# A two-block transformer kernel on one core: function table loaded early, small row tables moved later, last store in two halves

## The reference, cut to what matters

```
h = rmsnorm(x, g_pre_mix)                       # start of block 1
proj = h @ w_in                                 # split into q, six k/v parts, gates, ...
kb = k[:, blk] + pos[None, None, :, None, :]    # compressed keys and values: position rows added
...
x = x + rmsnorm(ff, mlp_norm_post[1])           # end of block 2; x is the output
```

## Time and profile before

| | us |
|---|---|
| median of 3 runs | 2114.84 |
| lowest, highest | 2113.89, 2118.77 |
| the profiled execution | 2114.21 |
| its span, first to last instruction | 2112.5 |
| PE busy in the span | 2076.6 |
| DVE busy | 1055.0 |
| ACT busy | 831.1 |
| POOL busy | 256.2 |

### The profile page before, as it was taken

The page is one execution under the profiler, slowest core; times in us unless marked ns, Lnnn a source line. Parts: engine busy times, 40 slices in busy tenths (PEclk is TensorE's granted clock), DMA queues, the critical chain, the costliest instruction groups (busy, mean ns, idle before and its releaser), DMA issues.

```text
span 2112.5 us, 27223 instructions
## 1 busy us (share of the span) xinstructions
PE 2076.6 (98%) x10878; PEld 1717.9 (81%) x10878; DVE 1055.0 (50%) x1782; ACT 831.1 (39%) x1539; POOL 256.2 (12%) x306
## 2 busy tenths in 40 slices
PE   8999999999999999999999999999999999999998
PEld 7987567888887888888888888888877779888887
DVE  5543756565555344665666433333655555334333
ACT  4154765343333234423335322322445554223222
POOL 7400000000000000223321000000433111000000
PEclk9999999999999999999999999999999999999999
DMA  6335512333333222222112223222332222332222
GB/s 163 84 116 87 68 40 81 100 101 100 86 95 100 100 100 90 90 67 74 60 61 80 94 97 100 100 100 100 110 102 89 70 81 90 100 98 94 89 99 80
DMA packets 172347, 191.95 MB, mean 91 GB/s; under 512 B 22882, under 2 KB 141965, under 8 KB 172221
## 3 DMA queue, kind: packets, MB, share of 16 engines
q1 hardware_dynamic: 168301, 176.30, 26.3%
q0 software_dynamic: 3904, 13.90, 3.5%
q10 hardware_dynamic: 16, 0.00, 0.0%
HBM read 182.84 MB, written 7.34 MB: 90 GB/s over the span
## 4 chain that ended last, share of the span: by engine, by line
PE 92%; DVE 4%; ACT 2%; issue 1%; POOL 1%; DMA 0%; POOLq 0%; ACTq 0%; DVEq 0%
PE bank L2463 25%; PE bank L2361 12%; PE bank L2362 12%; PE bank L2363 12%; PE bank L2400 2%; PE bank L2919 2%; PE bank L2401 2%; PE bank L2402 2%; PE bank L2954 1%; PE bank L2956 1%; PE bank L2955 1%; PE bank L2975 1%; PE bank L2615 1%; PE bank L2977 1%; PE bank L2976 1%; PE bank L2631 1%
## 5 line engine op out<-in xcount | busy, mean ns | idle before, releaser
L1577 DVE TENSOR_TENSOR WHL<-raw,WHL 128x1024 fp32r<-128x1024 f32 x309 | 393.5, 1275 | 475.8 <-ACT WHL L967 475.6
L967 ACT ACTIVATE WHL<-raw 128x1024 fp32r<-128x1024 f32 x309 | 325.2, 1054 | 526.5 <-PE bank L2463 338.1
L2361 PE MATMUL bank<-HXh,WHL 128*128 128x512 f32 x1136 | 448.5, 395 | 0.0
L2363 PE MATMUL bank<-HXh,WHL 128*128 128x512 f32 x1136 | 443.6, 390 | 0.0
L2362 PE MATMUL bank<-HXl,WHL 128*128 128x512 f32 x960 | 374.2, 390 | 0.0
L2463 PE MATMUL bank<-WHL,HXh 128*128 128x512 f32 x1344 | 362.3, 390 | 0.0
L2463 PEld LDWEIGHTS bank<-WHL,HXh 128*128 128x128 f32 x1344 | 251.6, 188 | 52.8 <-issue 1.2
L2361 PEld LDWEIGHTS bank<-HXh,WHL 128*128 128x128 f32 x1136 | 213.8, 188 | 48.2 <-issue 4.0
L2363 PEld LDWEIGHTS bank<-HXh,WHL 128*128 128x128 f32 x1136 | 213.6, 188 | 45.1
L2362 PEld LDWEIGHTS bank<-HXl,WHL 128*128 128x128 f32 x960 | 180.5, 188 | 36.0
L2463 PE MATMUL bank<-WHL,HXl 128*128 128x512 f32 x672 | 208.6, 390 | 0.0
(11 more groups left out here) (327 smaller groups left out, 3257.7 us busy)
## 6 DMA issues: line engine op xcount, KB each, us to landing
raw<-in_mlp_w_up_dram SPq DMA_DIRECT2D x64, 512.0 KB, 4.7
raw<-in_mlp_w_down_dram SPq DMA_DIRECT2D x64, 512.0 KB, 4.2
raw<-in_w_up_dram SPq DMA_DIRECT2D x44, 512.0 KB, 5.1
raw<-in_a_w_in_dram SPq DMA_DIRECT2D x32, 512.0 KB, 4.5
raw<-in_w_in_dram SPq DMA_DIRECT2D x24, 512.0 KB, 4.6
raw<-in_w_down_dram SPq DMA_DIRECT2D x22, 512.0 KB, 4.2
raw<-in_w_kv_dram SPq DMA_DIRECT2D x16, 512.0 KB, 4.2
rel_dram<-GB POOLq DMA_DIRECT2D x1, 5120.0 KB, 54.8
```

The source lines that it names most:

```text
L967: return a.activation(dst, src, ACT.Copy, **k)
L1577: v.tensor_tensor(dst(1), src, dst(0).bitcast(F32), ALU.subtract).then_inc(w_lo, 1)
L2361: m.matmul(b[:, :], w[0][:, k, :], x[0][:, k, :], start=(k == 0), stop=False)
L2363: return m.matmul(b[:, :], w[1][:, k, :], x[0][:, k, :], start=False, stop=(k == KD - 1))
```

## The change

Five edits in three places.

1. ScalarE makes a one-column Square into a scratch tile (`junk`) right after `consts`, before it waits for X. The wait for `consts` leaves `norm_tile`.
2. SyncE issues `row_tables()` ahead of slot 3 and no longer ahead of slot 2.
3. TensorE makes the five transposes of `stage` after the four groups of `q` and no longer before them.
4. VectorE splits up to `unit_at["q", 3]` (unit 5) before it waits for those transposes. The copy, the four additions and `split(unit_at["q", 3] + HL)` (units 6 to 8) stand behind as before.
5. The sum of the last tile is made by column halves, and each half is stored by a transfer of its own.

```diff
+        table_in, last_half = sem("table_in"), sem("last_half")
...
             for n, (name, i, parts) in enumerate(slots[:last]):
-                if n == RAW:
+                if n == RAW + 1:
                     row_tables()
...
-            for tt in range(TT):
+            for tt in range(TT - 1):
                 sp.wait_ge(x_ready, 4 * (len(NORMS) - 1) + tt + 1)
                 sp.dma_start(out[0, tt * P:(tt + 1) * P, :], X[:, tt, :]).then_inc(stored, 16)
-            sp.wait_ge(stored, 16 * TT)
+            sp.wait_ge(last_half, 1)
+            sp.dma_start(out[0, T - P:T, 0:HALF], X[:, TT - 1, 0:HALF]).then_inc(stored, 16)
+            sp.wait_ge(x_ready, 4 * len(NORMS))
+            sp.dma_start(out[0, T - P:T, HALF:D], X[:, TT - 1, HALF:D]).then_inc(stored, 16)
+            sp.wait_ge(stored, 16 * (TT + 1))
...
                 if n == 0:
-                    if tt == 0:
-                        act.wait_ge(consts, 1)
                     act.wait_ge(x_tile_in[tt], 16)
...
+            act.wait_ge(consts, 1)
+            a.activation(junk[:, 0:1], negh[:, 0:1], ACT.Square).then_inc(table_in, 1)
             norm_tile(0, 0)
...
-                    v.scalar_tensor_tensor(out=X[:, tt, :], in0=yg[:, tt % 2, :], scalar=yr[:, tt:tt + 1],
-                                           in1=X[:, tt, :], op0=ALU.mult, op1=ALU.add).then_inc(x_ready, 1)
+                    for c in (slice(0, HALF), slice(HALF, D)) if (r, tt) == (6, TT - 1) else (slice(0, D),):
+                        v.scalar_tensor_tensor(out=X[:, tt, c], in0=yg[:, tt % 2, c], scalar=yr[:, tt:tt + 1],
+                                               in1=X[:, tt, c], op0=ALU.mult,
+                                               op1=ALU.add).then_inc(x_ready if c.stop == D else last_half, 1)
...
             split(unit_at["kv01", 1] + HL)

+            split(unit_at["q", 3])
             vec.wait_ge(ps_free["act"], 2)
             vec.wait_ge(consts, 1)
             cols_copy(1)
...
             half_product(0, 1, 1)
+            split_features("q", 4, None, pair(True))
             pe.wait_ge(rows_in, 16 * N_ROWS)
             c = 0
             for i, n in enumerate((C_CONV, CUT, CUT, CMP_L, CMP_L)):
                 ins = m.transpose(bank[4][:, c:c + n], stage[0:n, i, :], ident[0:n, 0:n])
                 c += n
             ins.then_inc(cols_psum, 1)
-            split_features("q", 4, None, pair(True))
             split_features("kv24", 2, None, pair(True))
```

## The result

| | kernel before | changed kernel |
|---|---|---|
| median of 8 runs each | 2113.97 us | 2121.55 us |
| range of the runs | 2112.02 to 2118.77 | 2120.64 to 2126.88 |
| profiled execution, its span | 2114.21, 2112.5 | 2120.64, 2118.9 |

The ratio is 1.0040 (95% interval 1.0031 to 1.0049): the change costs 7.6 us. The forecast was 2120.4, 5.6 above the median known then.

What follows compares the result with a forecast made beforehand. TensorE, busy 98% of the span, was taken as the bound. Start -0.9, new wait with GpSimd and clock +7.9, earlier waits -0.8, end -0.6: +5.6, from 2114.84 to 2120.4 us, range 2117.0 to 2124.5.

Steps and rivals of the forecast that it cites:

- The bound and the place of the loss: Whole kernel: TensorE bounds it, busy 98% of the span; it would wait ahead of `kv24` for VectorE's unit 6.
- The wait: TensorE ahead of `kv24`: 5.9 us for copy, additions and one subtraction, plus 0.7 for GpSimd; sign: 6 to 7 idle.
- The third rival: VectorE's additions before `kv24`: two or more GpSimd selects get between; wait near 10, +9.2 us, time 2124.0; chance 0.14.
- The clock: TensorE after the `kv24` wait: granted clock falls to half somewhere from 51 to 58; +1.3 us, bounds 0 and 2.5.
- What is late next: TensorE after `kv24`: no further unit late, first earlier wait gone and half the second; -0.8 us, bounds -1.1 and 0.
- the old waits: TensorE's waits for VectorE in the kernel before: 0.58 us for unit 9, 0.52 for the evacuation of `kv35`.
- Edit 1: Start, ScalarE: the 1.28 us table load goes under X's transfer; first evacuation at about 10.3; -0.9 us, bounds -1.3 and 0.
- Edit 2: SyncE's queue: slot 3 issued at about 29.5, its first use at 40.21, so no wait; 0 us.
- Edit 5: End, last sum and store in halves: half the transfer saves 0.65, second sum some 0.05 later; -0.6 us, bounds -0.7 and -0.3.
- The total: Whole kernel: all terms sum to +5.6 us, from 2114.84 to 2120.4; chance 0.52.
- The bare wait: Rival at `kv24`: wait just 5.9, no loss to GpSimd or clock; +3.3 us, time 2118.1, within no change; chance 0.25.

Runs made afterwards that it cites:

- the middle alone: Changed kernel without the early table load and the split store at the end (edits 2, 3 and 4 only): 2123.81 us, ratio 1.0050.
- a wait at unit 9: Changed kernel with VectorE splitting up to unit 8, not only unit 5, before it waits for the transposes: 2115.72 us, ratio 1.0013.
- the masks moved: Changed kernel with GpSimd starting its mask loop only when unit 6 is split: 2117.83 us, ratio 1.0021.
- filled kernels: Changed kernel with 30 or 38 unread 512-column products on TensorE between the transposes and the wait for unit 6: 2121.53 and 2121.77 us.
- the two ends alone: Kernel before with only the early table load and the split store at the end (edits 1 and 5): 2112.63 us, ratio 0.9994.

## Why the prediction was right, and where its terms were off

- **The bound and the place of the loss** were right. The loss is one wait of TensorE ahead of `kv24`, ended by VectorE's subtraction of unit 6, as forecast from the order of the queue; moving the units ahead of the wait removed it.
- **The wait** was the mis-sized term. Forecast 5.9 and 0.7 for GpSimd, measured 9.03, outside the 6 to 7 us that the prediction gave as its sign. The bare part measured 5.49, GpSimd's 3.5 and not 0.7. I had judged by the four additions of the earlier trace rows, which hardly lost beside GpSimd (one took 1.35, the others 1.00 to 1.02); but what ran beside them there was tensor_scalar work, not selects. The row that did bear on it was unit 7's 3.56 beside a select. The third rival had this mechanism and its size, at 4: its wait of near 10 is closer to 9.03 than my 6.6, and its +9.2 a little closer to the measured +7.6 than my +5.6. Its argument against itself, that GpSimd would have the longest selects behind it, was wrong: GpSimd itself came 3.5 us earlier than before (its select of 3.67 at 40.96 in place of 44.46), and the two longest mask selects, 2.13 and 2.12, fell on the additions.
- **The clock**: forecast 1.3, read 2.2 to 2.3 in the trace. The fall came as said, between 51 and 58. The sums of the spans need it, here (1.8 with the middle alone) and in the kernels with a wait at unit 9 and with the masks moved (1.7 each). But neither kernel that kept TensorE busy had a lower median than the changed one: 0.9 to 1.1 came back as waits, and the rest is the second fall, which both filled traces have and the changed kernel's has not. Whether the medians hold the same difference I can't say from one trace each. With intervals of about 3 us either way for the filled kernels, how much of the 2.2 counts in the median stays open.
- **What is late next**: nothing, as forecast; the old waits were both gone and gave 1.5 and not 0.8, since each cost more than its idle time.
- **Edit 1**: 1.3 at the first evacuation and not 0.9. I took the landings from before; after, the three tiles of X came 0.3 to 0.4 sooner than those landings say, and the Squares with them. By the last `kv01` group it was 1.5, 1.2 to 1.3 in five other kernels, and 0.2 in the one whose first products ran at 0.41 until 15.6.
- **Edit 2**: 0, as forecast, but slot 3 was issued at 27.15 and not at about 29.5: in the kernel before it came at 27.02, right behind the subtraction of 25.77 to 27.00 that frees its place, so the new order moved it by 0.1. **Edit 5**: 0.4 to 0.5 and not 0.6; half the bytes took 0.5 off the landing and not 0.65, and the second issue came 0.13 later and not 0.05.
- **The total** (+5.6 forecast, +7.6 measured) is off by the GpSimd share and the clock, 3.4 too low together, less gains that were 1.2 larger (start, old waits, end). That 2120.4 lies only 1.2 below the measured 2121.55 is in part luck: it starts from a median of 2114.84, and eight runs put the kernel before at 2113.97. The bare wait, which was to end as no change, needs a GpSimd that stands still: forced to, the kernel stood at +4.1.

## What to carry to other kernels

Before a wait is put into an in-order queue, list what stands behind it and who needs that first; here 4.6 us of work that nobody waited for was put ahead of a unit that the bound engine wanted at once. Work of that kind belongs behind the last thing the bound engine needs, at a place where GpSimd has no selects to run and nothing that is wanted soon: the same copy and additions were 6.9 us of a wait at 48 and cost nothing at 72. Price an operation of VectorE beside GpSimd by a row with the same kind of GpSimd instruction, not by any row in which GpSimd was busy.

## What the runs showed of the hardware that I had not expected

- GpSimd's selects on 128x256 cost by their shape of mask: in the changed kernel's loop 2.13, 1.44, 1.40, 0.65, 0.52 and 0.45 us for one and the same number of elements, some of them perhaps held up by VectorE. An addition of VectorE beside the first ones took up to 2.26 in place of 0.98.
- It goes the other way too: GpSimd's four casts of 128x128 took 3.76 us beside the additions in place of 1.05, and its tensor_scalar of 128x512 took 2.27 beside them in the kernel before in place of 1.49.
- The half clock also came with TensorE busy throughout, behind a row of small products (129.8 to 133.0 in the kernel before). Seven of the nine traces have it there; the changed kernel's and that of the two ends alone have not.
- A wait of TensorE costs more than its idle time: the old waits of 0.58 and 0.52 were worth 1.5 together.
- At the start the product of 256 columns took 0.41 until 15.6 in the trace of the two ends alone and 0.28 from 11.25 on in the changed kernel's, while the windows give a granted clock of 1.00 for both; there the rate is to be read from the durations.
- A store of 256 KB landed 2.1 us after its issue, one of 512 KB 2.6 (medians of 2 and 3).
